# One transposition turn in every even head, and output products a tile later, in a fused SGU and sparse-attention block

## The reference

```
h    = rmsnorm(x);  proj = h @ w_in            # 3272 columns
a_u, a_v, a_z, b_q, b_k, b_v, b_z, i_q, i_k, i_w = split(proj)
ya   = gelu(a_u) * (W_sgu @ layernorm(gelu(a_v)) + b)       # 128-row blocks, 4 groups
idx  = sum_h relu(i_q[h] . layernorm(i_k)) * i_w[h]         # 8 indexer heads
sel  = top 256 of idx for each row, among the admissible keys
p[h] = softmax(q[h] . k / 8 - slope[h] * distance), over sel only   # 8 heads, one k and v
yb   = p @ v
out  = x + concat(rmsnorm(ya) * silu(a_z), rmsnorm(yb) * silu(b_z)) @ w_out
```

## Time and profile before

| | us |
| --- | --- |
| median of three timed runs | 568.47 (568.3 to 568.5) |
| the profiled execution | 568.53 |
| its span | 566.7 |
| TensorE busy (matmul, weight load) | 546.9, 463.5 |
| VectorE, ScalarE, GpSimd busy | 442.4, 371.4, 185.3 |
| start of the first group of probabilities in tiles 0, 2, 4, 6 | 320.14, 361.17, 412.68, 474.89 |

### The profile page before, as it was taken

The page is one execution under the profiler, slowest core; times in us unless marked ns, Lnnn a source line. Parts: engine busy times, 40 slices in busy tenths (PEclk is TensorE's granted clock), DMA queues, the critical chain, the costliest instruction groups (busy, mean ns, idle before and its releaser), DMA issues.

```text
span 566.7 us, 8941 instructions
## 1 busy us (share of the span) xinstructions
PE 546.9 (97%) x2974; PEld 463.5 (82%) x2974; DVE 442.4 (78%) x1105; ACT 371.4 (66%) x711; POOL 185.3 (33%) x287
## 2 busy tenths in 40 slices
PE   8999999999999999999999998989999999999997
PEld 8997788878888888887888886778788888888886
DVE  4775778899979998999879867787787788767631
ACT  5885767767997667878987558655555565646520
POOL 1760000014449996676220004741212031201130
PEclk9999999999999999999999999999999999999999
DMA  8623110013231111221112237111202111020122
GB/s 251 217 61 107 57 38 20 1 38 94 92 93 39 40 53 38 58 74 45 54 54 74 84 122 223 57 56 57 85 27 64 49 42 54 20 75 0 38 75 75
DMA packets 39982, 39.69 MB, mean 70 GB/s; under 512 B 6144, under 2 KB 28160, under 8 KB 39936
## 3 DMA queue, kind: packets, MB, share of 16 engines
q1 hardware_dynamic: 38416, 39.11, 22.9%
q10 hardware_dynamic: 1520, 0.01, 0.1%
HBM read 30.72 MB, written 8.39 MB: 69 GB/s over the span
## 4 chain that ended last, share of the span: by engine, by line
PE 75%; DVE 14%; ACT 5%; issue 3%; DMA 1%; POOL 1%; SPq 0%; ACTq 0%; DVEq 0%
PE ps_proj L1068 37%; PE ps_proj L1232 11%; PE ps_proj L1204 5%; PE ps_tp L1189 5%; PE ps_lg L1095 4%; PE ps_lg L1096 4%; PE ps_lg L1232 3%; DVE cand L1470 2%; DVE w_lo L1377 2%; DVE score L1423 1%; PE ps_tp L1153 1%; DVE xT_lo L1691 1%; PE ps_tp L1085 1%; DMA kvi_raw<-in_w_in_dram 1%; PE ps_tp L1225 1%
## 5 line engine op out<-in xcount | busy, mean ns | idle before, releaser
L1068 PE MATMUL ps_proj<-w_hi,xT_hi 128*128 128x512 f32 (+1 forms) x432 | 164.4, 381 | 1.3 <-DVE w_lo L1377 0.9
L1068 PE MATMUL ps_proj<-w_lo,xT_hi 128*128 128x512 f32 (+1 forms) x432 | 161.1, 373 | 0.0
L1068 PE MATMUL ps_proj<-w_hi,xT_lo 128*128 128x512 f32 (+1 forms) x432 | 161.1, 373 | 0.0
L911 ACT ACTIVATE ps_lg<-score,cand 128x768 f32<-128x768 f32 (+2 forms) x96 | 96.1, 1001 | 10.3 <-DVE cand L1470 10.3
L1068 PEld LDWEIGHTS ps_proj<-w_hi,xT_hi 128*128 128x128 f32 x432 | 81.4, 188 | 15.1 <-DVE w_lo L1377 2.1
L1068 PEld LDWEIGHTS ps_proj<-w_lo,xT_hi 128*128 128x128 f32 x432 | 81.4, 188 | 14.8
L1068 PEld LDWEIGHTS ps_proj<-w_hi,xT_lo 128*128 128x128 f32 x432 | 81.5, 189 | 12.2
L968 ACT CAST xT_hi<-ps_tp 128x512 fp32r<-128x512 f32 (+3 forms) x96 | 43.8, 483 | 57.7 <-PE ps_tp L1189 57.6
L1691 DVE TENSOR_TENSOR xT_lo<-ps_tp,xT_hi 128x512 fp32r<-128x512 f32 (+3 forms) x96 | 50.8, 553 | 31.2 <-ACT xT_hi L968 31.0
L1377 DVE SCALAR_TENSOR_TENSOR w_lo<-stage,g_in,w_hi 128x512 fp32r<-128x512 f32 x48 | 43.1, 906 | 10.0 <-ACT w_hi L771 9.2
L952 ACT ACTIVATE lo_f<-lo_f,negmax 128x128 f32<-128x128 f32 (+7 forms) x64 | 50.3, 785 | 0.2
(11 more groups left out here) (177 smaller groups left out, 1105.7 us busy)
## 6 DMA issues: line engine op xcount, KB each, us to landing
stage<-in_w_in_dram SPq DMA_DIRECT2D x48, 256.0 KB, 2.7
x_in<-in_x_dram SPq DMA_DIRECT2D x8, 512.0 KB, 4.8
lo_f<-in_x_dram SPq DMA_DIRECT2D x7, 512.0 KB, 4.0
out_dram<-lo_f SPq DMA_DIRECT2D x7, 512.0 KB, 3.5
q_scratch<-nat SPq DMA_DIRECT2D x8, 256.0 KB, 2.1
q_in<-q_scratch SPq DMA_DIRECT2D x8, 256.0 KB, 3.8
stage<-in_w_out_dram SPq DMA_DIRECT2D x8, 256.0 KB, 2.7
z_scratch<-nat SPq DMA_DIRECT2D x8, 256.0 KB, 2.0
```

Source lines behind the costliest of these rows:

```text
L911: act.activation(ps_lg[i % 2][:, 0:keys(t)], score[:, sc_off[t]:sc_off[t] + keys(t)], ACT.Sign, bias=cand[:, t:t + 1].bitcast(F32), scale= ...
L1068: mm = pe.matmul(ps_proj[u % 2][:, 0:n], a[:, k, rows], b[:, k, 0:n], start=(k == 0 and i == 0), stop=(k == KB - 1 and i == 2))
```

## The change

Turns move. Before, q was turned at head 2, the mixed rows of tile t - 1 at head 6, y at heads 5 and 1 (of the next tile). Now the mixed rows of tile t - 2 are turned at head 0, y at heads 6 and 2 and q at head 4, and q and y come ahead of the last background step of their head. The output products of a tile run a tile later, with two steps in every head. The gate's 32 steps are spread over 16 heads and the weights, gates, additions and selection steps move with them; of the right half's eight weight blocks GpSimd now splits 4 (6 before) and VectorE 4.

```
-        Q_AT, MIX_AT, YT_AT = 2, 6, (5, 1)
+        Q_AT, MIX_AT, YT_AT = 4, 0, (6, 2)
-                if h == MIX_AT and t > 0:
-                    tp_plan += [("m", t - 1, 0), ("m", t - 1, 1)]
+                if h == MIX_AT and t > 1:
+                    tp_plan += [("m", t - 2, 0), ("m", t - 2, 1)]
-        tp_plan += [("y", T - 1, 1), ("m", T - 1, 0), ("m", T - 1, 1)]
+        tp_plan += [("m", T - 2, 0), ("m", T - 2, 1), ("y", T - 1, 1), ("m", T - 1, 0), ("m", T - 1, 1)]
-        STEPS_BZ = [3] * 8 + [2] * 4
+        STEPS_BZ = [3] + [2] * 14 + [1]
-        W_FROM = len(STEPS_BZ)
-        BY_POOL = 6
+        FIRST_HALF_W_AT = {2: FREE, 5: FREE + 1, 9: FREE + 2, 12: FREE + 3}
+        W_AT = (16, 16, 17, 17, 20, 21, 22, 23)
+        BY_POOL = 4
...
@@ ScalarE
                     if m in last_units:
                         tanh_z(last_units[m])
-                        w_and(BZ, last_units[m])
-                    if W_FROM <= m < W_FROM + KB:
-                        hi_w(KB * O2 + m - W_FROM)
+                    if m in FIRST_HALF_W_AT:
+                        w_and(BZ, FIRST_HALF_W_AT[m])
+                    for k in range(KB):
+                        if W_AT[k] == m:
+                            hi_w(KB * O2 + k)
...
@@ TensorE
-            LAST_PV_BEHIND = 3
-            STEPS = {7: 3, 0: 3, 1: 2, 2: 2, 3: 2, 4: 2, 5: 1, 6: 1}
+            STEPS = 2
...
-                    if h == Q_AT and t + 1 < T:
-                        qT(t + 1)
-                    steps = STEPS[h]
-                    if m < 8 + MIX_AT:
-                        steps = STEPS_BZ[m] if m < len(STEPS_BZ) else 0
-                    for _ in range(steps):
+                    steps = STEPS_BZ[m] if m < len(STEPS_BZ) else STEPS
+                    for i in range(steps):
+                        if i == steps - 1:
+                            if h == Q_AT and t + 1 < T:
+                                qT(t + 1)
+                            if h == YT_AT[0]:
+                                turn_y(t, 0)
+                            if h == YT_AT[1] and t > 0:
+                                turn_y(t - 1, 1)
                         next(pending, None)
...
-                    if h == MIX_AT and t > 0:
-                        mT(t - 1, 0)
-                        mT(t - 1, 1)
-                        pending = out_steps(t - 1)
+                    if h == MIX_AT and t > 1:
+                        mT(t - 2, 0)
+                        mT(t - 2, 1)
+                        pending = out_steps(t - 2)
...
-            for _ in range(LAST_PV_BEHIND):
+            for _ in range(STEPS):
                 next(pending)
+            mT(T - 2, 0)
+            mT(T - 2, 1)
+            pending = out_steps(T - 2)
             pv(T * H // 2 - 1)
-            left = 2 * KB - STEPS[7] - LAST_PV_BEHIND
+            left = 2 * KB
...
@@ VectorE
-            LATE_AT = ((1, 3, 6), (6, 7), (1, 3, 6, 7))
+            LATE_AT = ((2, 4, 6), (2, 4, 6), (0, 2, 4, 6))
...
-                    if h == 1 and t > 1:
-                        add_res(t - 2, 0)
-                    if h == 6 and t > 1:
-                        add_res(t - 2, 1)
-                    if h == MIX_AT and t > 0:
-                        lo_mix(t - 1, 0)
-                        lo_mix(t - 1, 1)
+                    if h == MIX_AT and t > 2:
+                        add_res(t - 3, 1)
+                    if h == MIX_AT and t > 1:
+                        lo_mix(t - 2, 0)
+                        lo_mix(t - 2, 1)
                     if h == Q_AT and t + 1 < T:
                         lo_q(t + 1)
+                    if h == 4 and t > 1:
+                        add_res(t - 2, 0)
...
-                        lo_w(KB * O1 + last_units[m])
-                    if h == 2 and t > 0:
+                    if m in FIRST_HALF_W_AT:
+                        lo_w(KB * O1 + FIRST_HALF_W_AT[m])
+                    if h == 3 and t > 0:
                         y_sums(t - 1)
```

More of the change, by code:

```diff
@@ L1004, in _ @@
                     m = head_no(t, h)
-                    if h == MIX_AT and t > 0:
-                        hi_mix(t - 1)
+                    if h == MIX_AT and t > 1:
+                        hi_mix(t - 2)
                     if h == Q_AT and t + 1 < T:
@@ L1017, in _ @@
                         tanh_z(last_units[m])
-                        w_and(BZ, last_units[m])
-                    if W_FROM <= m < W_FROM + KB:
-                        hi_w(KB * O2 + m - W_FROM)
-                    if h == 2 and t > 0:
+                    if m in FIRST_HALF_W_AT:
[4 more added lines that the diff above has]
+                    if h == YT_AT[1] and t > 0:
                         y_square(t - 1)
+            hi_mix(T - 2)
             copy_yT(T - 1, 1)
@@ L1270, in _ @@
             scores(0, 1)
-            LAST_PV_BEHIND = 3
-            STEPS = {7: 3, 0: 3, 1: 2, 2: 2, 3: 2, 4: 2, 5: 1, 6: 1}
-            assert sum(STEPS.values()) == 2 * KB
+            STEPS = 2
+            assert STEPS * H == 2 * KB
             pending = last_projections()
@@ L1277, in _ @@
                     m = head_no(t, h)
-                    if h == Q_AT and t + 1 < T:
-                        qT(t + 1)
-                    steps = STEPS[h]
-                    if m < 8 + MIX_AT:
-                        steps = STEPS_BZ[m] if m < len(STEPS_BZ) else 0
-                    for _ in range(steps):
-                        next(pending, None)
[L1285 to L1288, removed]
-                    if h == MIX_AT and t > 0:
-                        mT(t - 1, 0)
-                        mT(t - 1, 1)
-                        pending = out_steps(t - 1)
+                    steps = STEPS_BZ[m] if m < len(STEPS_BZ) else STEPS
[5 more added lines that the diff above has]
+                                turn_y(t, 0)
+                            if h == YT_AT[1] and t > 0:
+                                turn_y(t - 1, 1)
+                        next(pending, None)
+                    if h == MIX_AT and t > 1:
+                        mT(t - 2, 0)
+                        mT(t - 2, 1)
+                        pending = out_steps(t - 2)
                     if m % 2 == 0 and m > 0:
@@ L1762, in _ @@
                         twice_silu(last_units[m])
-                        lo_w(KB * O1 + last_units[m])
-                    if h == 2 and t > 0:
+                    if m in FIRST_HALF_W_AT:
+                        lo_w(KB * O1 + FIRST_HALF_W_AT[m])
+                    if h == 3 and t > 0:
                         y_sums(t - 1)
-                    if W_FROM + BY_POOL <= m < W_FROM + KB:
-                        if m == W_FROM + BY_POOL:
+                    if m in W_AT[BY_POOL:]:
+                        if m == W_AT[BY_POOL]:
                             dve.wait_ge(w_lo_done, KB * O2 + BY_POOL)
-                        lo_w(KB * O2 + m - W_FROM)
+                        lo_w(KB * O2 + W_AT.index(m))
                     if m < 2:
@@ L1773, in _ @@
                         next(late, None)
+            add_res(T - 3, 1)
+            lo_mix(T - 2, 0)
+            lo_mix(T - 2, 1)
             y_rows(T - 1, 1)
```

## The result

The changed kernel takes 565.2 us (565.1 to 565.3), the one before 568.5: a ratio of 0.9942 (95%: 0.9930 to 0.9954), 3.3 us less. The forecast was 561.6, 6.9 less. The direction and the range hold; the gain is 3.3 us for 6.9. The profiled execution took 565.30 for a span of 563.5.

The account below looks back on a forecast made before the run. The prediction took TensorE as the bound, with its standing time to be won: 568.5 less 15.4 us of old pauses plus 8.5 of new ones gives 561.6 us, range 558.9 to 566.0.

Parts of the forecast that it names:

- the eight pauses of y: Odd heads 5 and 1, tiles 4 to 7: second group waits for y's sum, 0.8 or 0.5 us each; all go.
- The last head's wait: Last head, 2 steps instead of 3: TensorE reaches the last groups before the exponential is ready, a pause of 0.65 us.
- Rival C: Odd heads of tiles 4 to 7: ScalarE's exponential becomes the wait, 3.2 us more, 564.8 us; chance 0.11.
- the term of 8.5 for new pauses: Whole kernel: new TensorE pauses of 7.55 us at listed heads, with late starts 8.5 us.
- the late starts that were charged apart: Behind some ten new pauses: 0.1 us each for the late start of what follows, not placed at any head.
- the walk: Heads 0 to 24 followed instruction by instruction with profiled durations: 5.35 us of pauses in tiles 0 to 2.
- tile 5, head 2: The y turn waits for its bank, behind the 1024-column scan and additions at head 0: a pause of 0.9 us.
- The weight at head 24: Head 24: second step waits 1.85 us for the last weight's split, the group behind the mixed rows adds 0.3.
- Heads 16 to 18: Head 16: second turn of mixed rows waits 0.9 us for head 15's subtraction, the group behind it 0.4.
- Later than 60 us (the walk says 58): Sign that the forecast is wrong: groups of head 24 later than 60 us after those of head 0.
- Rival A: Tiles 0 to 2: VectorE paces them at an 83% share, 5.3 us of pauses for 3.2, 563.7 us; chance 0.15.
- The rule on GpSimd and VectorE: GpSimd and a two-SBUF-input VectorE operation lock each other out; head 16's scan delays a GpSimd weight up to 1.75 us, sum unchanged.

Follow-up runs that it names:

- e15: e4 with y turned in odd heads 5 and 1, ahead of the last step, instead of even heads 6 and 2: 571.81 us, 0 of its masks or q cut.
- e12: e4 with output steps dealt unevenly, 3, 2, 2, 2, 2, 1, 1, 3 in heads 0 to 7, instead of two per head: 569.63 us.
- e5: e4 with the turns of q and y behind the last step of their even head, not ahead of it: 565.33 us.
- e4: The changed kernel with the last two of the right output half's eight weight blocks made one head earlier: 563.17 us.
- e7: The kernel before with only y's turns, in their odd heads, moved ahead of the head's last step: 567.00 us.
- e16: e4 with selection steps of tiles 5 to 7 on 128 columns and q's operations on 32 (masks and q incomplete): 556.99 us.
- e2: The changed kernel with selection steps in odd heads instead of even ones: 569.99 us.
- e3: The changed kernel, but in tiles 2 and 3 VectorE adds the first output half before it reads q: 565.35 us.
- e13: e4 with ScalarE's and VectorE's readings of the turned q on 32 of 128 columns (q incomplete): 562.03 us.
- e14: e4 with the 1024-column scan moved to head 6 of tile 5 and tile 7's other selection steps to heads 0, 2, 4 of tile 6: 562.88 us.
- e6: The changed kernel with three steps in the last head and one behind the loop instead of two: 566.4 us.
- e9: The changed kernel with selection steps respread, three a tile up to tile 4, moving the 1024-column scan out of head 0 of tile 5: 566.97 us.

## Why the prediction was right in its direction and wrong in its size

**Right: what goes.** No group waits for the sum of y any more; the eight pauses of y are gone. In the new arrangement e15 (even heads, 7.8 us), e12 (two steps in every head, 6.5) and e5 (the place ahead of the last step, 2.2) each show a condition of it. Each of the first two undone alone costs more than e4's whole gain over the kernel before (5.3 us), and the third alone, in the old order (e7), is worth 1.5. They are not parts with a price each; the prediction priced the even turn and the step together, and was right to.

**Right: most of the new places.** Of the places of the list only head 4 shows no pause. The last head's wait was forecast as 0.65 and measured as 0.65, with the exponential as releaser. Rival C (0.4 for the exponential in the odd heads of tiles 4 to 7) did not occur; but at heads 5 and 13, where ScalarE's exponential stands behind its copies of q and y, it holds TensorE for 0.3 each, start to start. Tile 0 is 4.4 us shorter (some 4 forecast), with VectorE at 83%.

**Wrong: the term of 8.5 for new pauses, which measured 12.95.** The failed step is the price of the queue in even heads, above all in tiles 3 to 5. Of the 4.5, heads 0 to 24 have 2.0 (7.39 for 5.35), heads 29 to 46 have 3.2 (4.78 for 1.55), and the late starts that were charged apart take 0.95 off. Three parts:

1. *The queue in even heads.* The sum charges 3.45 at heads 4 to 14, 21 to 46 (0.95 + 0.95 + 0.45 + 0.2 + 0.9); measured, these places hold 7.7 (1.50 + 1.44 + 1.62 + 1.00 + 2.16). e16, which leaves the order as it is and shortens q and the selection steps, gets 6.2 back, and at these places some 1.3 is left. This is the mechanism of the walk, mis-sized by about 4. One place can be read at tile 5, head 2. VectorE's rows:

```profile
440.00 0.95 DVE L1686 CUSTOM_DVE_ANT_0 lo_f<-ps_lg,score 128x768 f32<-128x768 f32 x1
...
440.88 2.29 DVE L1530 TENSOR_TENSOR_SCAN rank<-eq 128x1024 f16<-128x1024 int8 x1
443.20 1.02 DVE L1696 TENSOR_TENSOR xT_lo<-ps_tp,xT_hi 128x512 fp32r<-128x512 f32 x2
```

   TensorE is ready for the turn when its last product has started, 442.45 + 0.23 = 442.68, 1.8 us after the scan's start. The pause is 444.03 - 442.68 = 1.35 for 0.9. The scan's length was right (2.29 for 2.28); which of the start times was off can't be told, since the forecast gives none for this head. TensorE's own work was not the error: without pauses it took 61.97 - 7.39 = 54.6 in heads 0 to 24, for the 54.8 of the forecast. The walk ended at head 24, and behind it the forecast priced single places: the group of head 32 (0.29), the turns of heads 34, 38 and 46 (0.25, 0.18, 0.12), the q turns of heads 36 and 44 (0.18, 0.44) and the group behind q at head 44 (0.25, called nothing "from tile 5 on") were in no term, 1.7 together.

2. *The weight at head 24*: 1.82 and 0.87 for 1.85 and 0.3. The split was timed well. What was undersized is what stands around it: 0.56 is the group behind the mixed rows, waiting for their remainder, and the rest late starts. e4 took 2.0 of the 2.7 away.

3. *Heads 16 to 18*: 1.76 for 1.3, the wait at the turn of mixed rows itself as forecast (0.91 idle for 0.9).

**A sign of the forecast was set wrong.** "Later than 60 us (the walk says 58)" for the groups of head 24 leaves out the 2.15 of head 24, which stand ahead of those groups: 54.8 + 5.35 is 60.2. Measured is 61.97, so the walk was 1.8 short there and not 4.

**Rival A was right in its number.** With the 2.15 of head 24 its pauses for this stretch are 7.45, and 7.39 was measured, with VectorE at 51.63 of 61.97, 83%, the share that A set. Its 563.7 lies 1.5 below because it changed nothing in tiles 3 to 5. But its reason, a ceiling on VectorE's share, does not hold: e4 has the same stretch in 59.86 us with VectorE at 51.41, 86%, and e2 gives VectorE the same work in another order and is 4.8 slower. It is the position of work in the queue; a share only sums it up.

**The rule on GpSimd and VectorE.** GpSimd's scaling of a weight takes 1.76 us beside the scan of 768 columns and 0.69 without; VectorE's own split takes 1.22 beside GpSimd's two-input operation and 0.75 without it. The first two rows are GpSimd's scaling (the scan runs from 357.87 to 359.62), the third its addition; then come VectorE's split beside that addition and alone:

```profile
358.37 1.76 POOL L733 TENSOR_SCALAR hi_f<-hi_f,g_out 128x512 f32<-128x512 f32 x1 [8.54 <-ACT w_hi L772]
361.50 0.69 POOL L733 TENSOR_SCALAR hi_f<-hi_f,g_out 128x512 f32<-128x512 f32 x1
...
368.92 1.30 POOL L710 TENSOR_TENSOR lo_f<-hi_f,lo_f 128x512 f32<-128x512 f32 x1
```

```profile
369.55 1.22 DVE L1382 SCALAR_TENSOR_TENSOR w_lo<-lo_f,g_out,w_hi 128x512 fp32r<-128x512 f32 x1
...
378.46 0.75 DVE L1382 SCALAR_TENSOR_TENSOR w_lo<-lo_f,g_out,w_hi 128x512 fp32r<-128x512 f32 x1
```

That agrees with the Trainium skill (SBUF — State Buffer, SBUF: two separate sides) in both directions. No pause of TensorE was traced to it.

**Open.** How the 4.5 divide exactly between places mis-sized and places left out was not separated by a run, nor q's part between ScalarE and VectorE. Whether a mix of e4's weights with a q read by ScalarE alone would take the rest wasn't tried.

## What to carry to other kernels

In an in-order queue a pause that is removed at one wait often comes back at the next: e3 moved one by a head for a gain of 0, e13 and e14 kept 1.1 and 0.3. It stays away where the queue has room at the new place, as in e4 (2.0). Price a reorder by walking every stretch to its end with start-to-start times, and where the walk stops, add a range and not zero. Two releases that share a pair of buffers need work between them that is longer than all that stands in the consumer's queue, not only its one instruction; put the request in front of a step and where the most other products lie.

## What was not expected of the hardware

In part of the executions of some kernels the granted clock was halved for some 3.4 us right behind a long pause of TensorE (1.65, 1.76 and 2.23 us idle in the traces of e6, e9 and e15). In e6, after the same wait at head 24 that the changed kernel has, against the changed kernel itself (windows as above):

```profile
380.30:383.50 3.20, 3.20 (x17) 3.20 (x16) 2.08 (x3) 1.30 (x3) 0.00 (x0) 0.50 0.33 101
```

```profile
380.30:383.50 3.20, 2.80 (x22) 2.49 (x21) 2.10 (x4) 2.29 (x5) 0.00 (x0) 1.00 0.37 112
```

The window has 17 matmuls in e6 (first row) and 22 in the changed kernel: 0.50 of the clock is the lower of its two levels, 1.2 GHz. What e6's TensorE did before it fell:

```profile
379.33 0.50 PE L1236 MATMUL ps_proj<-w_hi,mixT_hi 128*128 128x512 f32 x1 [1.65 <-DVE w_lo L1382]
...
380.15 1.05 PE L1229 MATMUL ps_tp<-ident,y_a 128*128 128x128 f32 x4
```

The four executions of e6 with it took 566.4 to 566.6, the one without 565.1: 1.3 us. e15 shows the same behind its wait of 2.23 (572.6 with, 571.0 without, 1.6 us). The pause alone does not bring it: the changed kernel has the 1.65 too and showed it in none of its four executions, and e2 and e5 have one of 1.78 idle and showed it in none of ten and four. e3, with the same 1.65, showed it in one of four. The kernels whose longest pause was under 1.4 idle have a mean granted clock of 0.999 or 1.00 in every execution, against 0.996 or 0.997 where it fell. So a long pause can cost twice, and e4 takes away the longest.
